# A hybrid decoder layer: small triangular blocks of the recurrence on GpSimd one chunk ahead, and a route stage with paired columns and a compact list

## The reference, cut to what matters

```python
def step(state, inp):                                  # 8 heads of 64, one token after the other
    r_t, w_t, k_t, v_t, kk_t, a_t = inp
    sa = jnp.einsum('bhvk,bhk->bhv', state, -kk_t)
    state = (state * w_t[:, :, None, :]
             + sa[..., None] * (kk_t * a_t)[:, :, None, :]
             + v_t[..., None] * k_t[:, :, None, :])
    return state, jnp.einsum('bhvk,bhk->bhv', state, r_t)
...
h = rms_norm(x, norm_ffn_g)
logits = h @ w_router + b_router                       # 32 experts
top, index = lax.top_k(logits, 4)
gate = softmax(top)
y = sum over the 4 experts of gate * (clamped_swiglu(h @ w1[e] + b1[e]) @ w2[e] + b2[e])
```

## Time and profile before

| | us |
|---|---|
| median of 3 runs | 3333.78 (3332.63 to 3338.41) |
| the profiled execution's own time | 3337.43 |
| its span, first to last instruction | 3335.8 |
| TensorE busy | 2915.2 (87%) |
| VectorE busy | 1133.8 (34%) |
| ScalarE busy | 660.2 (20%) |
| GpSimd busy | 514.2 (15%) |
| mean granted clock of TensorE | 0.936 |

### The profile page before, as it was taken

The page is one execution under the profiler, slowest core; times in us unless marked ns, Lnnn a source line. Parts: engine busy times, 40 slices in busy tenths (PEclk is TensorE's granted clock), DMA queues, the critical chain, the costliest instruction groups (busy, mean ns, idle before and its releaser), DMA issues. The chain is left out here.

```text
span 3335.8 us, 54999 instructions
## 1 busy us (share of the span) xinstructions
PE 2915.2 (87%) x21052; PEld 2740.4 (82%) x21053; DVE 1133.8 (34%) x2508; ACT 660.2 (20%) x1258; POOL 514.2 (15%) x584
## 2 busy tenths in 40 slices
PE   8899898789999397979299999999999999999990
PEld 7876674688888396879199999999999999999990
DVE  2129223454443531335223222232223223223227
ACT  3129213112211322322011111111111111111111
POOL 0000003122222000003311211211211221121203
PEclk9999898899999698989599999999999999999995
DMA  6100110000000302022588877888888888887877
GB/s 226 35 25 1 51 36 22 1 0 0 0 0 0 107 2 76 7 59 57 178 309 284 285 267 253 294 284 290 287 298 285 289 294 289 290 281 260 283 248 266
DMA packets 320783, 543.73 MB, mean 163 GB/s; under 512 B 23457, under 2 KB 102177, under 8 KB 320673
## 3 DMA queue, kind: packets, MB, share of 16 engines
q1 hardware_dynamic: 301344, 499.78, 43.9%
q0 software_dynamic: 19360, 42.87, 4.3%
HBM read 506.01 MB, written 36.59 MB: 163 GB/s over the span
## 5 line engine op out<-in xcount | busy, mean ns | idle before, releaser
L2279 PE MATMUL experts_up<-experts_xs,g_pieces 128*128 128x144 f32 (+1 forms) x8192 | 1035.8, 290 | 99.0 <-DVE experts_xs L2208 60.4
L2279 PEld LDWEIGHTS experts_up<-experts_xs,g_pieces 128*128 128x128 f32 x8192 | 1029.1, 197 | 106.1 <-issue 106.1
L2302 PE MATMUL experts_down<-experts_hs,g_across 128*128 128x144 f32 (+1 forms) x3072 | 394.5, 289 | 3.7 <-issue 2.7
L2302 PEld LDWEIGHTS experts_down<-experts_hs,g_across 128*128 128x128 f32 x3072 | 387.6, 190 | 7.5 <-issue 7.4
L2161 POOL DMA_INDIRECT experts_x<-h_rows,experts_index x198 | 192.2, 971 | 1148.3 <-DVE experts_xs L2208 1093.4
L2238 DVE TENSOR_SCALAR experts_glu<-experts_up,experts_bias 128x176 f32<-128x176 f32 x256 | 102.3, 400 | 713.2 <-PE experts_up L2279 713.2
L2188 ACT ACTIVATE experts_sig<-experts_glu 128x352 f32<-128x352 f32 x128 | 63.6, 497 | 967.9 <-DVE experts_lin L2240 967.9
L2195 ACT ACTIVATE experts_yT<-experts_down,experts_bias 128x176 f32<-128x176 f32 x256 | 99.5, 406 | 394.8 <-DMA diff_qk_raw<-in_w_in_dram 142.9
L1017 POOL TENSOR_TENSOR chunk_part<-chunk_corr,rwkv_level_mask 128x1024 f32<-128x1024 f32 x56 | 119.2, 2129 | 351.3 <-DVE chunk_corr L1106 188.2
L2229 DVE COPY experts_bias<-g_bias 128x24 f32 x32 | 5.8, 182 | 400.7 <-ACT experts_yT L2195 400.7
L2291 PE MATMUL experts_down<-experts_hs,g_across 128*128 128x144 f32 (+1 forms) x1024 | 133.2, 289 | 0.0
(11 more groups left out here) (403 smaller groups left out, 4397.6 us busy)
## 6 DMA issues: line engine op xcount, KB each, us to landing
g_pieces<-in_w_dram SPq DMA_DIRECT2D x132, 2048.0 KB, 8.0
g_across<-in_w_dram SPq DMA_DIRECT2D x64, 2048.0 KB, 8.0
y_rows<-experts_y SPq DMA_DIRECT2D x132, 192.0 KB, 3.8
g_across<-in_w_ckv_dram SPq DMA_DIRECT2D x8, 1024.0 KB, 10.3
rkv_raw<-in_w_in_dram SPq DMA_DIRECT2D x13, 512.0 KB, 3.9
diff_qk_raw<-in_w_in_dram SPq DMA_DIRECT2D x9, 512.0 KB, 3.9
cross_q_raw<-in_w_cq_dram SPq DMA_DIRECT2D x9, 512.0 KB, 4.1
m_u<-in_x_dram SPq DMA_DIRECT2D x8, 512.0 KB, 9.7
```

Source lines behind the costliest of these rows:

```text
L2279: ins = pe.matmul(up[:, u % 4, l * N:l * N + w], raw[c][:, k, at:at + 255:2], xs[:, k, 0:w], start=(k == 0), stop=(k == 7), skip_group_che ...
L2302: ins = pe.matmul(down[:, n % 4, 0:w], raw[4 + n // 4][:, k, (n % 4) * P:(n % 4 + 1) * P], hs[:, k, 0:w], start=(k == 0), stop=(k == 7), s ...
```

## The change

**Recurrence.** The diagonal blocks of 16x16 are inverted apart from the rest, and levels 0 to 3 leave PE. The b-a correlations of chunk i+1 (`ab`) are made in chunk i, by eight PE products (`products_ab`) behind the first half of level 5, and masked by VectorE. A new row on SyncE (`relay`) stores them in DRAM (`lower_rows`), loads the 64 diagonal blocks (8 groups x 8 heads) onto 64 partitions, waits for GpSimd, stores the inverted blocks (`solved_rows`) and loads them in a compact form. GpSimd inverts the blocks in `solve_blocks`, 29 operations in a row, at the end of its row of chunk i, ahead of its copy of v for chunk i+1. In chunk i+1 VectorE spreads the compact form to the block diagonal (`inv`) and transposes it (`invT`). Levels 4, 5 and 6 stay as they were. The masks take 384 columns per head where they took 512, and a's correlations with b are no longer in them; the wait of PE on the scaled state moves from before the correlations to the right side. For chunk 0 the new products, the relay and the blocks are done ahead of the loop. `mixed` (PSUM) now also holds the new products.

**Route.** Column parts 2 and 3 are interleaved tile by tile (`order`, `PAIRED`), and what follows for a tile runs one step later than before. The list is laid out by windows: an entry's row is (rank // 176) x 32 x 176 + expert x 176 + rank % 176, so that neighbouring experts' pieces are 176 entries apart instead of 1024, at the price of two small VectorE operations more per tile (`share`, `listed`). The four regrouping copies become one of 1024 elements. The four loads of the first expert's w1 are issued in the route stage, behind the row stores and the last product of `w_co`, for which `high` and `low` are put under `pieces`.

The diff, cut to its core:

```diff
-LEVELS = 7
+SIDE, GROUPS = 16, 8
+LEVELS = (4, 5, 6)
+lower = nc.dram_tensor("lower_rows", [P, H, P], F32).ap()
+solved = nc.dram_tensor("solved_rows", [P, H, SIDE], F32).ap()
...
+@block.sync
+def _(sp):
+    def relay(n, first):
+        sp.wait_ge(ahead_dve.sem, ahead_dve.value("ab1", n))
+        sp.dma_start(lower, ab[:]).then_inc(lower_out, 16)
+        sp.wait_ge(lower_out, n * 16 + 16)
+        for s in range(GROUPS):
+            at = slice(s * SIDE, (s + 1) * SIDE)
+            sp.dma_start(block16[s * H:(s + 1) * H], lower[at, :, at].rearrange("j h c -> h j c")).then_inc(block_in, 16)
+        sp.wait_ge(ahead_pool.sem, ahead_pool.value(f"row{SIDE - 2}", n))
+        if not first:
+            sp.wait_ge(dve_steps.sem, dve_steps.value("inv", n - 1))
+        for s in range(GROUPS):
+            at = slice(s * SIDE, (s + 1) * SIDE)
+            sp.dma_start(solved[at, :, :].rearrange("r h c -> h r c"), small[s * H:(s + 1) * H]).then_inc(solved_out, 16)
+        sp.wait_ge(solved_out, n * (16 * GROUPS) + 16 * GROUPS)
+        sp.dma_start(compact[:], solved).then_inc(compact_in, 16)
+    relay(0, True)
+    with sp.Fori(0, NCH - 1) as i:
+        relay(i + 1, False)
+
...
+def solve_blocks(n):
+    ahead_pool.round()
+    pool.wait_ge(block_in, n * (16 * GROUPS) + 16 * GROUPS)
+
+    pool.wait_ge(solved_out, n * (16 * GROUPS))
+    pool.wait_ge(ahead_pool.sem, ahead_pool.so_far(n))
+    pool.tensor_tensor(small[:], block16[:].rearrange("p j i -> p i j"), eye16[:], ALU.add).then_inc(*ahead_pool.step("start"))
+    for k in range(1, SIDE - 1):
+        rest = SIDE - 1 - k
+        product = outer[:, 0:rest * k].rearrange("p (i c) -> p i c", c=k)
+        pool.wait_ge(ahead_pool.sem, ahead_pool.so_far(n))
+        pool.tensor_tensor(product, block16[:, k, k + 1:SIDE].unsqueeze(2).to_broadcast([GROUPS * H, rest, k]),
+                           small[:, k, 0:k].unsqueeze(1).to_broadcast([GROUPS * H, rest, k]),
+                           ALU.mult).then_inc(*ahead_pool.step(f"outer{k}"))
+        pool.wait_ge(ahead_pool.sem, ahead_pool.so_far(n))
+        pool.tensor_tensor(small[:, k + 1:SIDE, 0:k], small[:, k + 1:SIDE, 0:k], product,
+                           ALU.add).then_inc(*ahead_pool.step(f"row{k}"))
...
     pool.tensor_copy(vc[:], u[:, 8:12, now]).then_inc(*pool_steps.step("v"))
-    pool.wait_ge(dve_steps.sem, dve_steps.value(f"mask{H - 1}", i))
-    for l in range(LEVELS):
-        if l >= 1:
-
-            pool.wait_ge(pe_steps.sem, pe_steps.value("l0_1" if l == 1 else f"l{l - 1}_p1", i))
-            if l == 1:
-                pool.wait_ge(dve_steps.sem, dve_steps.value("l0_s1", i))
+    pool.wait_ge(ahead_dve.sem, ahead_dve.value("ab1", i))
+    for n, l in enumerate(LEVELS):
+        if n == 0:
+            pool.wait_ge(pe_steps.sem, pe_steps.value("l6_p1", i - 1))
+        else:
+            pool.wait_ge(pe_steps.sem, pe_steps.value(f"l{l - 1}_p1", i))
         pool.wait_ge(pool_steps.sem, pool_steps.so_far(i))
         pool.tensor_tensor(
-            part[:], corr[:, :, 0, :],
-            level_mask[:, l, :].unsqueeze(1).to_broadcast([P, H, P]), ALU.mult).then_inc(*pool_steps.step(f"part{l}"))
+            part[:], ab[:],
+            level_mask[:, n, :].unsqueeze(1).to_broadcast([P, H, P]), ALU.mult).then_inc(*pool_steps.step(f"part{l}"))
+    if more:
+        solve_blocks(i + 1)
+solve_blocks(0)
 all_chunks(pool, chunk)
...
-    dve.tensor_tensor(kc[:], k, power[:, 1], ALU.mult).then_inc(*ahead_dve.step("k"))
     dve.wait_ge(ahead_dve.sem, ahead_dve.so_far(i))
     dve.tensor_tensor(bc[:], bc[:], power[:, 1], ALU.mult).then_inc(*ahead_dve.step("b"))
+    dve.scalar_tensor_tensor(ar[:, :, 0, :], kk, -1.0, lag, ALU.mult, ALU.mult).then_inc(*ahead_dve.step("a"))
 elif part == 3:
-    dve.wait_ge(ahead_dve.sem, ahead_dve.so_far(i))
+    for g in groups:
+        dve.wait_ge(ahead_pe.sem, ahead_pe.value(f"ab{g}", i))
+        dve.tensor_tensor(ab[:].rearrange("p (c two) n -> p two c n", two=2)[:, g], mixed[:, g, :].rearrange("p (h n) -> p h n", n=P),
+                          corr_mask[:, 0, :].unsqueeze(1).to_broadcast([P, 4, P]), ALU.mult).then_inc(*ahead_dve.step(f"ab{g}"))
...
-    dve.tensor_tensor(corr[:, h], pairs[:, h % 2, :].rearrange("p (c n) -> p c n", n=P),
-                      corr_mask[:], ALU.mult).then_inc(*dve_steps.step(f"mask{h}"))
+    dve.tensor_tensor(corr[:, h], pairs[:, h % 2, 0:3 * P].rearrange("p (c n) -> p c n", n=P),
+                      corr_mask[:, 1:4], ALU.mult).then_inc(*dve_steps.step(f"mask{h}"))
+
+dve.wait_ge(compact_in, i * 16 + 16)
+dve.tensor_tensor(inv[:].rearrange("p h (s c) -> p h s c", c=SIDE),
+                  compact[:].unsqueeze(2).to_broadcast([P, H, GROUPS, SIDE]),
+                  own[:].unsqueeze(1).unsqueeze(3).to_broadcast([P, H, GROUPS, SIDE]), ALU.mult).then_inc(*dve_steps.step("inv"))
+dve.wait_ge(dve_steps.sem, dve_steps.so_far(i))
+dve.transpose(invT[:].rearrange("p h n -> p (h n)"), inv[:].rearrange("p h n -> p (h n)")).then_inc(*dve_steps.step("invT"))
 dve.wait_ge(pe_steps.sem, pe_steps.value("bonus", i))
...
-if more and l <= 3:
-    prepare(i + 1, l)
+if more and l == LEVELS[0]:
+    prepare(i + 1, 2)
+
+    dve.wait_ge(pool_steps.sem, pool_steps.value(f"part{LEVELS[-1]}", i))
+    prepare(i + 1, 3)
+if more and l == LEVELS[1]:
+    prepare(i + 1, 4)
...
+def products_ab(n):
+
+    ahead_pe.round()
+    pe.wait_ge(ahead_dve.sem, ahead_dve.value("a", n))
+    for h in range(H):
+        rows, c = slice(64 * (h % 2), 64 * (h % 2) + 64), h // 2
+        ins = pe.matmul(mixed[:, h % 2, c * P:(c + 1) * P], bc[rows, c, :], ar[rows, c, 0, :],
+                        start=(c == 0), stop=(c == CT - 1), skip_group_check=True)
+        if c == CT - 1:
+            ins.then_inc(*ahead_pe.step(f"ab{h % 2}"))
...
-pe.wait_ge(dve_steps.sem, dve_steps.value("state_in", i))
+pe.wait_ge(dve_steps.sem, dve_steps.value("r", i))
+pe.wait_ge(dve_steps.sem, dve_steps.value("scale1", i - 1))
 for h in range(H):
...
-    pe.matmul(pairs[:, h % 2, 0:256], bc[rows, c, :], both, start=True, stop=False, skip_group_check=True)
-    pe.matmul(pairs[:, h % 2, 256:512], kc[rows, c, :], both, start=False, stop=True,
+    pe.matmul(pairs[:, h % 2, 0:P], bc[rows, c, :], ar[rows, c, 1, :], start=True, stop=False, skip_group_check=True)
+    pe.matmul(pairs[:, h % 2, P:3 * P], kc[rows, c, :], both, start=False, stop=True,
               skip_group_check=True).then_inc(*pe_steps.step(f"corr{h}"))
 
 pe.wait_ge(act_steps.sem, act_steps.value("b", i))
-pe.wait_ge(pool_steps.sem, pool_steps.value("part0", i))
-for g in groups:
-    for j in range(4):
-        ins = pe.matmul(straight[:, g, j * P:(j + 1) * P], part[:, g * 4 + j, :], C.ident[:],
-                        start=(j == 0), stop=(j == 3), skip_group_check=True)
-    ins.then_inc(*pe_steps.step(f"l0_{g}"))
-
 pe.wait_ge(act_steps.sem, act_steps.value("y", i - 1))
+pe.wait_ge(dve_steps.sem, dve_steps.value(f"mask{H - 1}", i))
 for c in range(CT):
     pe.matmul(mixed[:, 0, c * P:(c + 1) * P], ar[:, c, 0, :], state[:, c, :], start=(c == 0),
...
+if n == 1 and more:
+    pe.wait_ge(act_steps.sem, act_steps.value("rhs", i))
+    products_ab(i + 1)
+if n == 0:
+    pe.wait_ge(dve_steps.sem, dve_steps.value("bonus", i))
 for g in groups:
...
+if more:
+    pe.wait_ge(ahead_dve.sem, ahead_dve.value("ab1", i + 1))
...
+pe.sem_inc(ahead_pe.sem, ahead_pe.start)
+products_ab(0)
 all_chunks(pe, chunk)
...
-ROOM = T_ALL
-LISTED = -(-(NE * ROOM + SLOTS) // P) * P
+LISTED = -(-(-(-T_ALL // WINDOW) * NE * WINDOW + SLOTS) // P) * P
...
+order = [(c, t) for c in range(PAIRED) for t in range(TT)]
+for s in range(TT + 1):
+    order += [(PAIRED, s)] if s < TT else []
+    order += [(LAST, s - 1)] if s >= 1 else []
...
     sp.wait_ge(regrouped, t + 1)
     sp.dma_start(h_rows[t * P:(t + 1) * P, :], quarters[:, t % 2, :]).then_inc(rows_out[t % 2], 16)
+sp.wait_ge(pe_steps.sem, pe_steps.value(cell(LAST, TT - 1)))
+for c in range(4):
+    sp.dma_start(pieces[:, c], I["w1"][0][0, :, c * 512:(c + 1) * 512]
+                 .rearrange("(k p) n -> p k n", p=P)).then_inc(loaded[c], 16)
...
-dve.tensor_tensor(place[:, t % 2, :], rank[:, t % 2, :], room[:], ALU.add).then_inc(*dve_steps.step(f"place{t}"))
+
+dve.tensor_scalar(share[:, t % 2, :], rank[:, t % 2, :], 1.0 / WINDOW, -(WINDOW - 1) / (2 * WINDOW),
+                  ALU.mult, ALU.add).then_inc(*dve_steps.step(f"share{t}"))
+dve.tensor_tensor(place[:, t, :], rank[:, t % 2, :], room[:], ALU.add).then_inc(*dve_steps.step(f"place{t}"))
 follows()
-dve.tensor_tensor(spot[:, t % 2], chosen[:, t], place[:, t % 2, :].unsqueeze(1).to_broadcast([P, TOPK, NE]),
+dve.scalar_tensor_tensor(listed[:, t % 2, :], share[:, t % 2, :], float((NE - 1) * WINDOW), place[:, t, :],
+                         ALU.mult, ALU.add).then_inc(*dve_steps.step(f"listed{t}"))
...
-        weights_low(c + 2)
+    weights_low(c + 2)
 for s in steps_of:
     if s < TT:
-        add(LAST, s)
+        add(PAIRED, s)
```

(21 more changed lines are left out.)

210 lines of the change are left out of this document (118 added, 92 removed).

## The result

| | us |
|---|---|
| before, median of 4 runs | 3333.41 (3332.63 to 3338.41) |
| changed, median of 4 runs | 3196.44 (3191.28 to 3201.38) |
| ratio | 0.9584, 95% interval 0.9565 to 0.9603 |
| forecast | 3244, range 3200 to 3305 |

The profiled execution of the changed kernel is the 3191.28 one, 5.2 under its median, and that of the kernel before lies 4.0 above its own, so the two traces differ by 146.1 (spans 3335.8 and 3189.7).

What follows compares the result with a forecast made beforehand. TensorE (PE), busy 2915.2 of 3335.8 us, was taken to bound the kernel. From 3337.43, recurrence -73.8 and route -16.1 gave 3247.5; less 3.65 to the median, 3243.9, say 3244 us, range 3200 to 3305.

Steps and rivals of the forecast that it cites:

- The mechanism: Recurrence: the relay through GpSimd's copy of v sets the chunk; PE idles 9.6 us before each and starts at low clock.
- PE's own path: Recurrence: PE's work in one chunk, counted from its first transpose, ends at 40.1 us, before the relay does.
- The relay's legs: Recurrence, per chunk: 25.4 to the masks' end, store 4.5, block loads 6.5, solve 12.6, copy of v 0.7; sum 49.7 us.
- the first relay: Recurrence, ahead of chunk 0: nothing covers it, so the first transpose comes at 634.6 instead of 609.02, 25.6 us later.
- The hindrance by VectorE: Recurrence, GpSimd's solve: VectorE operations in between hold it up some 1.5 us a chunk; by the port rule alone, nothing.
- The stretch at the route's end: Before the experts, no engine running: 23.17 us falls to 14, -8.8 us; ends 0 and -18.
- rival B: Route's end: only the tail without work goes, -18 us in place of -8.8, giving 3235 us; chance 0.17.
- The w1 loads: Experts' start: moving these four loads away shortens GpSimd's wait for the first index load, -2.7 us, between 0 and 5.
- The pairing: Route: interleaved column parts spread the first tiles' lists, so GpSimd's last indirect DMA ends 4.6 us earlier.
- Rival A: Recurrence: relay pieces at their low ends, 42.6 us a chunk, first chunk at 629, stage -129 us; chance 0.13.
- D: Recurrence, slower rival: GpSimd's small operations cost 0.75 us each, solve 25.2, +101 us, 3345; chance 0.08 with all its like.
- C: Recurrence rival: storing the solved blocks as 1024 64-byte pieces takes 18 us, not 6.5; +70 us, 3314; chance 0.12.

## Why the prediction was wrong, point by point

**The mechanism was right.** The relay ends behind GpSimd's copy of v, PE waits for it and starts at the low clock in every chunk but one, and the compact load comes in time. Moving v and lengthening the solve both show it. PE's own path is 38.75 us (716.67 to 755.42), 40.1 forecast.

**The relay's legs were mis-sized, and that is the error.** 49.7 forecast, 43.9 measured: in the chunk shown the store was 1.9 too long, the block loads 1.6, the solve 1.5, and the rest cancels; that is 5.0, and the mean chunk is another 0.8 shorter. Times seven, 41 us; 6.7 more in the first relay (634.6 forecast, 627.90 measured, 4.2 of it again the store and the loads); with the last chunk 48.2 in all, -122.0 for -73.8. The rows that I had chosen for the store were the output stores, which run beside others; the landing of a lone 512 KB store is the fastest of those eight, 2.6. For the block loads I added an issue of 0.5 each where a run of eight has 0.36. The hindrance by VectorE, 1.5 in the sum, is about 1; the case that it be nothing, for want of VectorE operations with two SBUF inputs in the solve, didn't come, since L1171 and L1174 fall there.

**The stretch at the route's end** was taken in the middle of its ends, 14 left; it is 9.55, and the pitch of 4096 bytes is the cause of what went (rival B, right). Without the w1 loads it is 4.3, near the lower end of 4.9. No row before told the two ends apart, so the middle was a guess. Its sum is also off a little: 14 us left make -9.1 and not -8.8.

**The w1 loads** were given -2.7; at their place they bring -3.8, and the stretch pays 4.7 in return. I had written that they could get in the writes' way and had allowed a few us for it without taking them from the sum. Net: nothing.

**The pairing** was given -4.6 (its two rows give 4.5), and GpSimd's end did come 3.2 earlier against the products; but the pairing alone brings about 1 us of order on GpSimd and nothing that the time shows. One regrouping copy of 1.05 us has taken the place of four, mostly of 1.4 to 1.6 together. That this is what shortened GpSimd's row fits, but no run has the copies alone.

**The range.** Rival A (pitch 42.6, start 629) was nearly exact in the recurrence, and B in the route, and both hold at once: 3337.4 - 129 - 18 - 7 = 3183 before the median's offset. I had them as exclusive cases with 0.13 and 0.17, and ended the range at 3200, where A holds only half way: A alone at its low ends, with the route as forecast, is 3337.4 - 129 - 16.1 - 3.7 = 3189. Two low ends in two stages are independent, and the range had to reach both. D never came near: the small operations are at 0.20 to 0.29 where VectorE doesn't hinder them, 0.29 as the mean of all. C neither: the 1024 pieces of 64 bytes of the way back took 4.1 us with their issues, not 18.

**Open:** the recurrence alone gains 104.9 us in time where the trace pair has 122.0, and 9 us of the difference are in no trace; and with 4096 bytes beside the w1 loads GpSimd's row ended 13.6 us later, for a reason not found.
